# Moving 32 expert up projections ahead of the gate matrix, and all modulation chunks into the gate stage

## The chip, the cores and the metric

One core of one Trainium2 chip runs the whole program. The metric is the device time of one execution in microseconds (us).

## What is computed

Two transformer blocks run one after the other on 256 tokens of width 1024, in float32. The change touches the product-key expert layer (peer) at the end of the first block, and the modulation vectors of the second block:

```python
q = (xt @ w_q).astype(f32).reshape(T, PEER_HEADS, 2, PEER_DKEY // 2)
s1 = jnp.einsum('thd,kd->thk', q[:, :, 0], sub_k1.astype(f32))
s2 = jnp.einsum('thd,kd->thk', q[:, :, 1], sub_k2.astype(f32))
v1, i1 = lax.top_k(s1, PEER_TOPK)
v2, i2 = lax.top_k(s2, PEER_TOPK)
cand = (v1[..., :, None] + v2[..., None, :]).reshape(T, PEER_HEADS, PEER_TOPK * PEER_TOPK)
vals, ci = lax.top_k(cand, PEER_TOPK)
...
idx = jnp.take_along_axis(i1, ia, axis=-1) * PEER_NKEYS + jnp.take_along_axis(i2, ib, axis=-1)
gates = jax.nn.softmax(vals, axis=-1)
...
u = expert_u[ii]
h = jnp.einsum('tkd,td->tk', u, xx).astype(f32)
a = (jax.nn.gelu(h) * gg).astype(x.dtype)
return jnp.einsum('tk,tkd->td', a, expert_v[ii])
...
mod_x = (jax.nn.silu(c) @ w_ada[l] + b_ada[l])[:, None, :]
mod_c = (jax.nn.silu(c_ctx) @ w_ada[l] + b_ada[l])[None, None, :]
```

The kernel does not gather experts. It runs the layer densely: for each of the 128 values e of the first key, all 128 experts that share it are projected for all 256 tokens (an "up" product of 1024 by 128 experts), passed through gelu, multiplied by the gate matrix, which is zero where a token did not choose the expert, and multiplied with their value rows (a "down" product).

## The kernel before, in words

All weights come as one stream of 637 chunks of 128x1024 floats (512 KB), in a fixed order (`ORDER`). SyncE loads chunk c into slot c % 4 of the ring `RAW`; it issues a load when the chunk four places before it has been split (`lo_ready`), or, for the chunks of the modulation matrix ("ada", 72 chunks), when it has been multiplied (`chunk_done`). A chunk that is multiplied in two float32r parts is split first: ScalarE rounds it into `WH` (`split_hi`, L409), VectorE writes the rest into `WL` (`split_lo`, L786), and TensorE multiplies with three products per tile (`product`, L1316 to L1318 in a feature chunk, L1539 to L1541 in a down product). Each engine works through its own queue in program order, and semaphores join the queues. No scheduler is involved: the order is that of the code.

The stages around the change, in order of time:

- **Query stage**: 16 "wq" chunks and, between them, the key scores (L1457). VectorE does the splits of these chunks and, between them in the same loop, `top`, the top-16 searches of the first four of eight heads (`STG`, `CAND`, `IF`, `VAL` and `CIU` are its tiles). Heads 4 to 7 follow, two at a time.
- **Selection**: `EQ` compares and sums 2048 elements at a time and makes `SEL` (expert row, expert column and gate of each of 128 slots). During top-k and selection TensorE multiplies the first 40 ada chunks: two rows of conditioning vectors (`CS`) are stationary, 512 columns of weights move (L1478). ScalarE copies the sums to `MROW`, and TensorE turns them (L1486).
- **Gate stage**: `SEL` is turned and copied to `SLT`. In 32 units of 8 tokens VectorE builds one-hot matrices `OI` and `OJ` (L1061, L1064), GpSimd multiplies `OI` by the gates (L379), TensorE multiplies the two for each token (L1513), and ScalarE evicts 128x1024 to the gate matrix `G` (L580). Each unit also takes one of the last 32 ada chunks (four units to an `MROW` row).
- **Peer stage**: 128 pairs of an up chunk (24 products of 256 columns) and a down chunk (12 of 512 columns). The down sums stay in PSUM.

The four queues meet in a few lines, which the steps of the prediction name:

```python
with dve.Fori(0, 3) as it:
    step.begin(it, 11)
    for j in range(4):
        split_lo(C0["wq"] + j + 2, it, 4)
        if j:
            top(j - 1, it, 1, it * 2 + 2)
```

## Time and profile before

| | |
|---|---|
| median of 3 executions | 2290.24 us (2286.39 to 2290.87) |
| the profiled execution | 2286.94 us, its span 2285.1 us |
| mean granted TensorE clock | 0.985 of full speed |
| TensorE busy | 97% of the span |
| VectorE, ScalarE, GpSimd busy | 54%, 42%, 4% |
| chain that ended last | 88% on TensorE, 8% on VectorE |

The span runs from the first to the last instruction; the execution's own time is 1.8 us longer. Busy time of TensorE counts overlapping, pipelined products once, so a high share says that it was hardly ever without one, and not that it could not be faster. The chain is followed back from the last instruction: at each step to what released it.

### The profile page before, as it was taken

To read this page: it belongs to the slowest core of one execution; us is meant where nothing else is said; L and a number is where in the kernel's file an instruction comes from. 1 tells how busy PE (TensorE), PEld (TensorE's weight loads), DVE (VectorE), ACT (ScalarE), POOL (GpSimd) and SP (SyncE) were. 2 spreads that over 40 slices of the span, in tenths; PEclk is the share of its full clock that TensorE was granted. 3 is DMA by queue.
4 is the path that set the end of the run, shared out by engine and by line. 5 is a ranking of instruction groups with operands and counts; after the bars stand their busy time and mean duration, and the time that the engine had idled before them with its cause. 6 is when DMAs were issued, how large, how long until landed. Compare 5 with 4: busy or idle time off the path is not lost.

```text
span 2285.1 us, 37329 instructions
## 1 busy us (share of the span) xinstructions
PE 2206.0 (97%) x13410; PEld 1893.8 (83%) x13410; DVE 1242.4 (54%) x1820; ACT 956.4 (42%) x1312; POOL 92.8 (4%) x50
## 2 busy tenths in 40 slices
PE   8999898999999999999999999999899999999998
PEld 6999723559999999999998888878788889898997
DVE  4557888985555555555557433322644444255554
ACT  5644311234444444444455323212433335336653
POOL 0000002650000000000000000000000000000000
PEclk9999999999999999999999999999999999999999
DMA  6434365436555556555554322232233335254553
GB/s 215 138 131 144 113 221 194 132 129 199 187 189 184 188 188 202 187 189 184 188 189 149 111 92 92 97 100 96 70 103 100 110 111 192 91 187 146 181 188 101
DMA packets 95689, 343.14 MB, mean 150 GB/s; under 512 B 10930, under 2 KB 12594, under 8 KB 95252
## 3 DMA queue, kind: packets, MB, share of 16 engines
q1 hardware_dynamic: 94532, 337.35, 44.4%
q0 software_dynamic: 1104, 5.05, 0.7%
q8 instruction: 38, 0.62, 0.1%
q14 instruction: 15, 0.12, 0.0%
HBM read 341.31 MB, written 1.05 MB: 150 GB/s over the span
## 4 chain that ended last, share of the span: by engine, by line
PE 88%; DVE 8%; issue 2%; ACT 1%; DMA 0%; DVEq 0%; POOL 0%; ACTq 0%; POOLq 0%
PE ps L1316 19%; PE ps L1317 19%; PE ps L1318 19%; PE ps L1539 5%; PE ps L1540 5%; PE ps L1541 5%; PE ps L1513 3%; PE ps L1478 3%; PE ps L1347 2%; PE ps L1348 2%; PE ps L1349 2%; PE ps L1671 1%; PE ps L1356 1%; DVE WL L786 1%; PE ps L1720 1%
## 5 line engine op out<-in xcount | busy, mean ns | idle before, releaser
L786 DVE TENSOR_TENSOR WL<-RAW,WH 128x1024 fp32r<-128x1024 f32 x565 | 683.2, 1224 | 665.1 <-ACT WH L409 661.0
L1316 PE MATMUL ps<-XH,WH 128*128 128x256 f32 (+1 forms) x2648 | 803.2, 303 | 29.7 <-DVE WL L786 16.2
L409 ACT ACTIVATE WH<-RAW 128x1024 fp32r<-128x1024 f32 x565 | 586.4, 1055 | 538.2 <-PE ps L1318 342.1
L1317 PE MATMUL ps<-XL,WH 128*128 128x256 f32 (+1 forms) x2648 | 794.5, 300 | 0.0
L1318 PE MATMUL ps<-XH,WL 128*128 128x256 f32 (+1 forms) x2648 | 794.2, 300 | 0.0
L1316 PEld LDWEIGHTS ps<-XH,WH 128*128 128x128 f32 x2648 | 511.8, 193 | 58.0 <-issue 20.5
L1317 PEld LDWEIGHTS ps<-XL,WH 128*128 128x128 f32 x2648 | 512.8, 194 | 20.3 <-issue 1.2
L1318 PEld LDWEIGHTS ps<-XH,WL 128*128 128x128 f32 x2648 | 512.5, 194 | 14.5
L1539 PE MATMUL ps<-WH,AH 128*128 128x512 f32 x512 | 200.8, 392 | 0.0
L1540 PE MATMUL ps<-WH,AL 128*128 128x512 f32 x512 | 200.7, 392 | 0.0
L1541 PE MATMUL ps<-WL,AH 128*128 128x512 f32 x512 | 199.2, 389 | 0.0
L1478 PE MATMUL ps<-RAW,CS 128*2 128x512 f32 x288 | 131.6, 601 | 4.6 <-ACTq L556 3.8
L1316 PE MATMUL ps<-HIDH,WH 128*128 (+2 forms) x352 | 119.3, 339 | 4.3 <-DVE HIDL L1158 4.3
L1318 PE MATMUL ps<-HIDH,WL 128*128 (+2 forms) x352 | 118.8, 337 | 0.0
L1317 PE MATMUL ps<-HIDL,WH 128*128 (+2 forms) x352 | 118.8, 337 | 0.0
L1541 PEld LDWEIGHTS ps<-WL,AH 128*128 128x128 f32 x512 | 96.2, 188 | 21.0
L1539 PEld LDWEIGHTS ps<-WH,AH 128*128 128x128 f32 x512 | 96.6, 189 | 16.7
L1540 PEld LDWEIGHTS ps<-WH,AL 128*128 128x128 f32 x512 | 96.7, 189 | 15.3
L1154 DVE TENSOR_TENSOR HT<-TA,ps 128x512 f32<-128x512 f32 (+1 forms) x44 | 24.4, 555 | 141.7 <-PE ps L1318 138.6
L1478 PEld LDWEIGHTS ps<-RAW,CS 128*2 128x2 f32 x288 | 21.6, 84 | 87.9 <-issue 68.2
L379 POOL TENSOR_TENSOR OI<-OI,SLT 128x1024 f32<-128x1024 f32 x32 | 86.5, 2702 | 124.9 <-DVE OI L1061 124.9
L1513 PEld LDWEIGHTS ps<-OI,OJ 128*128 128x128 f32 x512 | 61.1, 196 | 36.7 <-issue 36.7
(255 smaller groups left out, 2257.4 us busy)
## 6 DMA issues: line engine op xcount, KB each, us to landing
RAW<-in_wstream SPq DMA_DIRECT2D x637, 512.0 KB, 3.8
H<-in_xT SPq DMA_DIRECT2D x1, 1024.0 KB, 4.8
CTX<-in_ctxT POOLq DMA_DIRECT2D x1, 1024.0 KB, 7.6
HX<-in_ctxT POOLq DMA_DIRECT2D x1, 1024.0 KB, 5.9
DIST<-in_dist POOLq DMA_DIRECT2D x1, 1024.0 KB, 5.2
out<-HX SPq DMA_DIRECT2D x2, 512.0 KB, 3.3
MASK<-in_mask POOLq DMA_DIRECT2D x1, 512.0 KB, 3.9
DFTL<-in_dftl POOLq DMA_DIRECT2D x1, 512.0 KB, 3.7
```

Source lines behind the costliest of these rows:

```text
L379: pool.tensor_tensor(OI[:, q, :, :], OI[:, q, :, :], SLT[:, 2, bass.ds(it * 16 + 8 * q, 8)].unsqueeze(2).to_broadcast([P, 8, P]), ALU.mult ...
L409: act.activation(WH[:, slot, :], RAW[:, slot, :], ACT.Copy).then_inc(hi_ready, 1)
L786: dve.tensor_tensor(WL[:, slot, :], RAW[:, slot, :], WH[:, slot, :].bitcast(F32), ALU.subtract).then_inc(lo_ready, 1)
L1316: pe.matmul(dst, wh, xh, start=start, stop=False, skip_group_check=not check)
L1317: pe.matmul(dst, wh, xl, start=False, stop=False, skip_group_check=not check)
L1318: return pe.matmul(dst, wl, xh, start=False, stop=stop, skip_group_check=not check)
L1347: pe.matmul(dst, xh[:, k, t], WH[:, slot, w], start=(k == 0), stop=False)
L1478: ins = pe.matmul(ps[0:2, bank, :], CS[:, k, :], RAW[:, c % 4, kk * 512:kk * 512 + 512], start=(k == 0), stop=(k == KB - 1))
L1513: ins = pe.matmul(ps[:, 2 * q + t // 4, (t % 4) * P:(t % 4) * P + P], OJ[:, q, t, :], OI[:, q, t, :], start=True, stop=True)
L1539: pe.matmul(dst, AH[:, e % 2, t], WH[:, c % 4, d], start=first, stop=False)
L1540: pe.matmul(dst, AL[:, e % 2, t], WH[:, c % 4, d], start=False, stop=False)
L1541: ins = pe.matmul(dst, AH[:, e % 2, t], WL[:, c % 4, d], start=False, stop=last)
```

## The change

The stream gets a new part, "pre", between "wq" and "ada": the up chunks of rows 96 to 127. TensorE multiplies them during top-k and selection (`pre_up`), and ScalarE puts the gelu of each straight into its row of `G`. In the gate stage ScalarE evicts only rows 0 to 95, and VectorE multiplies the evicted sums of rows 96 to 127 into what `G` holds there (`gated_rows`). In the peer stage 32 down chunks come first, without ups, and then 96 pairs.

The splits of 14 wq chunks and 32 pre chunks leave VectorE for GpSimd. The multiplication of `OI` by the gates leaves GpSimd: VectorE builds `OI` in eight instructions per unit that compare and multiply in one.

All 72 ada chunks stand in the first 30 of the 32 gate units. The conditioning vectors are padded to 32 columns, and the eight products of a row go in turn to four groups of 32 PSUM partitions (each group holds two of the eight). After every fourth chunk the 128x512 sums are copied, turned by four full transposes (`turn_row`) and the four groups are added (`row_sum`).

```diff
-ADA1 = 10
-ADA2 = MODB // 4 - ADA1
-ADA_EXP = 6
-UNITS = T // 8 // ADA2
+PRE = 32
+PRE_ROW = NKEYS - PRE
+NE = NKEYS - PRE
+UNITS = T // 8
+ADA_UNITS = UNITS - 2
...
     ("wq", 16),
+    ("pre", PRE),
     ("ada", MODB),
-    ("peer", 256),
+    ("peer", 256 - PRE),
...
+def ada_through(n):
+    return min(MODB, (n + 1) * MODB // ADA_UNITS)
+def turn_after(done):
+    return done // 4 - 1 if done >= 6 and done % 4 == 2 else None
...
-            with pool.Fori(0, T // 16) as it:
-                for q in range(2):
-                    pool.wait_ge(s["oi_ready"], at(q + 1, 2, it))
-                    pool.tensor_tensor(OI[:, q, :, :], OI[:, q, :, :],
-                                       SLT[:, 2, bass.ds(it * 16 + 8 * q, 8)].unsqueeze(2).to_broadcast([P, 8, P]),
-                                       ALU.mult).then_inc(s["gi_ready"], 1)
-            pool.wait_ge(chunk_done, C0["peer"] + 3 + 2 * 63 + 1)
+            pool.wait_ge(s["pool_consts"], 4)
+            pool.memset(CS[:, :, :], 0.0).then_inc(s["cs_zeroed"], 1)
+            pool.wait_ge(lo_ready, C0["wq"] + 2)
+            for c in range(C0["wq"] + 2, ADA):
+                pool.wait_ge(hi_ready, c + 1)
+                pool.tensor_tensor(WL[:, c % 4, :], RAW[:, c % 4, :], WH[:, c % 4, :].bitcast(F32),
+                                   ALU.subtract).then_inc(lo_ready, 1)
...
+            for i in range(PRE):
+                c = C0["pre"] + i
+                if i and c + 2 < ADA:
+                    split_hi(c + 2)
+                act.wait_ge(chunk_done, c + 1)
+                act.activation(G[:, PRE_ROW + i, :], ps[:, (U_PRE + i) % 4, 0:T],
+                               ACT.Gelu_apprx_tanh).then_inc(ring_evac, 1)
+                if i == 20:
+                    act.wait_ge(s["vals_ready"], 1)
+                    act.activation(VAL[:, :, :, :], VAL[:, :, :, :], ACT.Exp).then_inc(s["val_exp"], 1)
+                if i == PRE - 5:
+                    act.wait_ge(s["slots_turned"], 1)
+                    act.activation(SLT[:, 0:2, :], ps[:, 4, :].rearrange("p (a t) -> p a t", t=T), ACT.Copy)
+                    act.activation(SLT[:, 2, :], ps[:, 5, 0:T], ACT.Copy).then_inc(s["slots_ready"], 1)
...
+            for n in range(UNITS):
+                act.wait_ge(s["onehot_used"], n + 3)
+                act.activation(G[:, 0:PRE_ROW, 8 * n:8 * n + 8],
+                               ps[:, 2 * (n % 2):2 * (n % 2) + 2, :].rearrange("p b (t i) -> p i (b t)", t=4)[:, 0:PRE_ROW, :],
+                               ACT.Copy).then_inc(s["g_ready"], 1)
+                while done < MODB // 4 and ada_through(n) >= 4 * done + 4:
+                    act.wait_ge(chunk_done, ADA + 4 * done + 4)
+                    if done >= 2:
+                        act.wait_ge(s["row_turned"], done - 1)
+                    act.activation(MROW[:, done % 2, :], ps[:, 6 + done % 2, :], ACT.Copy).then_inc(s["mrow_ready"], 1)
+                    done += 1
...
             with dve.Fori(0, 3) as it:
                 step.begin(it, 11)
-                for j in range(4):
-                    split_lo(C0["wq"] + j + 2, it, 4)
-                    if j:
-                        top(j - 1, it, 1, it * 2 + 2)
+                for part in range(3):
+                    top(part, it, 1, it * 2 + 2)
                 step.end(3)
-            split_lo(ADA - 2)
-            split_lo(ADA - 1)
...
+            def onehots(n):
+                q, tok = n % 2, slice(8 * n, 8 * n + 8)
+                if n < 2:
+                    dve.wait_ge(chunk_done, ADA - 1 + n)
+                else:
+                    dve.wait_ge(s["onehot_used"], n + 1)
+                dve.tensor_tensor(OJ[q][:, :, :], IOTA[:, :].unsqueeze(1).to_broadcast(wide),
+                                  SLT[:, 1, tok].unsqueeze(2).to_broadcast(wide), ALU.is_equal)
+                for t in range(8):
+                    own = slice(8 * n + t, 8 * n + t + 1)
+                    ins = dve.tensor_scalar(OI[q][:, t, :], IOTA[:, :], SLT[:, 0, own], SLT[:, 2, own],
+                                            ALU.is_equal, ALU.mult)
+                ins.then_inc(s["onehot_ready"], 1)
+            def gated_rows(n):
+                dve.wait_ge(s["g_ready"], n + 3)
+                g = G[:, PRE_ROW:NKEYS, 8 * n:8 * n + 8]
+                rows = ps[:, 2 * (n % 2):2 * (n % 2) + 2, :].rearrange("p b (t i) -> p i (b t)", t=4)
+                dve.tensor_tensor(g, rows[:, PRE_ROW:NKEYS, :], g, ALU.mult).then_inc(s["gm_ready"], 1)
+            def row_sum(g):
+                dve.wait_ge(s["row_turned"], g + 1)
+                turned = ps[:, 5, :].rearrange("p (i r c) -> p i r c", i=4, r=4)
+                dve.tensor_reduce(MOD[:, 4 * g:4 * g + 4, :], turned[:, :, :, 0:2].rearrange("p i r c -> p i c r"),
+                                  AXX, ALU.add).then_inc(s["row_summed"], 1)
+            dve.sem_inc(s["gm_ready"], 2)
+            onehots(0)
+            dve.wait_ge(ring_evac, U_GATES)
+            for n in range(UNITS):
+                if n + 1 < UNITS:
+                    onehots(n + 1)
+                gated_rows(n)
+                if n >= 1:
+                    for done in range(ada_through(n - 2) + 1 if n >= 2 else 1, ada_through(n - 1) + 1):
+                        if turn_after(done) is not None:
+                            row_sum(turn_after(done))
...
+            def pre_up(i, it=None):
+                bank_free(U_PRE + i, it)
+                feature_chunk(C0["pre"] + i, ps[:, (U_PRE + i) % 4, 0:T], XH, XL, it, 4)
+            with pe.Fori(0, PRE // 4 - 1) as it:
+                for i in range(4):
+                    pre_up(i, it)
             pe.wait_ge(s["sc_ready"], 16 + 4)
-            def mod_chunk(c, j, bank, it=None, n=0):
-                pe.wait_ge(landed[c % 4], at(16 * (c // 4 + 1), 4 * n, it))
-                for kk in range(2):
-                    k = 2 * j + kk
-                    ins = pe.matmul(ps[0:2, bank, :], CS[:, k, :], RAW[:, c % 4, kk * 512:kk * 512 + 512],
-                                    start=(k == 0), stop=(k == KB - 1))
-                ins.then_inc(chunk_done, 1)
-            def turn_rows(rows, m0, count):
-                for i in range(count):
-                    m = m0 + i
-                    ins = pe.transpose(ps[:, 7, 2 * m:2 * m + 2], rows[0:2, i * P:i * P + P], ID2[:, :])
-                return ins
-            with pe.Fori(0, ADA1 // 2) as it:
-                for q in range(2):
-                    pe.wait_ge(s["mrow_ready"], at(q + 1, 2, it))
-                    for j in range(4):
-                        mod_chunk(ADA + 4 * q + j, j, 6 + q, it, 8)
-            pe.wait_ge(s["id2_ready"], 1)
-            pe.wait_ge(s["mrow_ready"], ADA1 + 2)
-            turn_rows(MROW, 0, 4 * ADA1)
             pe.wait_ge(s["sel_ready"], 1)
             for n in range(3):
                 for tt in range(TT):
                     ins = pe.transpose(ps[:, 4 + n // 2, (n % 2) * T + tt * P:(n % 2) * T + tt * P + P],
-                                       SEL[:, n, tt, :, :].rearrange("p h k -> p (h k)"), IDENT[:, :])
+                                       SEL[:, n, tt, :, :].rearrange("p h k -> p (h k)"), IDP[:, :])
             ins.then_inc(s["slots_turned"], 1)
+            for i in range(PRE - 4, PRE):
+                pre_up(i)
+            def mod_chunk(i):
+                c, bank = ADA + i, 6 + (i // 4) % 2
+                pe.wait_ge(landed[c % 4], 16 * (c // 4 + 1))
+                for kk in range(2):
+                    k = 2 * (i % 4) + kk
+                    rows = slice(32 * (k % 4), 32 * (k % 4) + 32)
+                    ins = pe.matmul(ps[rows, bank, :], CS[:, k, :], RAW[:, c % 4, kk * 512:kk * 512 + 512],
+                                    start=(k < 4), stop=(k >= 4))
+                ins.then_inc(chunk_done, 1)
+            def turn_row(g):
+                pe.wait_ge(s["mrow_ready"], g + 1)
+                if g:
+                    pe.wait_ge(s["row_summed"], g)
+                for i in range(4):
+                    ins = pe.transpose(ps[:, 5, i * P:i * P + P], MROW[:, g % 2, i * P:i * P + P], IDP[:, :])
+                ins.then_inc(s["row_turned"], 1)
+            pe.wait_ge(s["cs_ready"], 1)
+            pe.wait_ge(s["const_landed"], 16 * 11)
+            pe.wait_ge(ring_evac, U_GATES)
             pe.sem_inc(s["onehot_used"], 2)
-            with pe.Fori(0, ADA2) as it:
-                for u in range(UNITS):
-                    q = u % 2
-                    pe.wait_ge(s["oj_ready"], at(u + 1, UNITS, it))
-                    pe.wait_ge(s["gi_ready"], at(u + 1, UNITS, it))
-                    pe.wait_ge(s["g_ready"], at(u + 1, UNITS, it))
-                    for t in range(8):
-                        ins = pe.matmul(ps[:, 2 * q + t // 4, (t % 4) * P:(t % 4) * P + P], OJ[:, q, t, :],
-                                        OI[:, q, t, :], start=True, stop=True)
-                    ins.then_inc(s["onehot_used"], 1)
-                    if u == 0:
-                        pe.wait_ge(s["mrow_ready"], at(ADA1 + 2, 1, it))
-                    if u % (UNITS // 4) == 0:
-                        j = u // (UNITS // 4)
-                        mod_chunk(ADA + 4 * ADA1 + j, j, 6, it, 4)
-            pe.wait_ge(s["mrow_ready"], MODB // 4 + 2)
-            turn_rows(MROW2, 4 * ADA1, 4 * ADA2).then_inc(s["mod_turned"], 1)
+            done = 0
+            for n in range(UNITS):
+                q = n % 2
+                pe.wait_ge(s["onehot_ready"], n + 1)
+                pe.wait_ge(s["g_ready"], n + 1)
+                pe.wait_ge(s["gm_ready"], n + 1)
+                for t in range(8):
+                    ins = pe.matmul(ps[:, 2 * q + t // 4, (t % 4) * P:(t % 4) * P + P], OJ[q][:, t, :], OI[q][:, t, :],
+                                    start=True, stop=True)
+                ins.then_inc(s["onehot_used"], 1)
+                while done < ada_through(n):
+                    if done >= 8 and done % 4 == 0:
+                        pe.wait_ge(s["mrow_ready"], done // 4 - 1)
+                    mod_chunk(done)
+                    done += 1
+                    if turn_after(done) is not None:
+                        turn_row(turn_after(done))
+            turn_row(MODB // 4 - 1)
...
             pe.wait_ge(s["mod_ready"], 1)
+            down(0, 0, PC + 2, first=True)
+            with pe.Fori(0, PRE // 4 - 1) as it:
+                for i in range(1, 5):
+                    down(i, i, PC + 2 + i, it, 4)
+            for i in range(PRE - 3, PRE):
+                down(i, i, PC + 2 + i)
             def pair(e, it=None):
                 if e >= 2:
                     pe.wait_ge(s["gated_ready"], at(e - 1, 4, it))
-                up(e + 2, PC + 2 + 2 * e, it)
-                down(e, PC + 3 + 2 * e, it, first=it is None and e == 0)
+                up(e + 2, PQ + 2 + 2 * e, it)
...
+    parts += [up[PRE_ROW:NKEYS]]
+    parts += [tokens(x["w_ada_2"][0][:, n:n + 512]) for n in range(0, N_MOD * D, 512)]
+    order = [up[0:1], up[1:2], down[PRE_ROW:NKEYS]]
+    for e in range(NE):
+        if e + 2 < NE:
```

**VectorE, the loop over the first heads.** Before, in the loop body (L786 is a split, L962 to L993 are steps of `top`):

```order
148 L785 REGISTER_ALU
149 L786 TENSOR_TENSOR WL<-RAW,WH 128x1024
150 L962 MAX V_102<-STG_101 128x8 x4
151 L105 REGISTER_ALU
152 L966 MAX_INDEX I_103<-V_102,STG_101 128x8 x4
153 L969 TENSOR_TENSOR CAND<-V_102 128x256 x2
```

Now:

```order
144 L996 MAX V_101<-STG_100 128x8 x4
145 L117 REGISTER_ALU
146 L1000 MAX_INDEX I_102<-V_101,STG_100 128x8 x4
147 L1003 TENSOR_TENSOR CAND<-V_101 128x256 x2
148 L117 REGISTER_ALU
149 L1008 ISA
150 L1008 COPY IF<-I_102 128x4x16
```

The split that stood ahead of the second search is gone from this queue, and so are the other three of each round. They stand on GpSimd, where before there was the product of `OI`:

```order
13 L384 MEMSET CS 128x256 [waits pool_consts]
14 L390 TENSOR_TENSOR WL<-RAW,WH 128x1024 [waits hi_ready,lo_ready]
15 L390 TENSOR_TENSOR WL<-RAW,WH 128x1024 [waits hi_ready] x45
16 L394 DMA CTX<-in_ctxT 128x2048 [waits chunk_done]
```

GpSimd now has 46 splits in a row, one behind the other, with nothing between them but the wait for ScalarE's half.

**TensorE, the gate stage.** Before, one turn of the loop, four units (L1513 one-hots, L1478 an ada chunk):

```order
1299 L1513 MATMUL ps<-OI,OJ 128x128 x8
1300 L1518 REGISTER_ALU
1301 L1475 ISA
1302 L1478 MATMUL ps<-RAW,CS 2x512 x2
1303 L1509 REGISTER_ALU
1304 L1513 MATMUL ps<-OI,OJ 128x128 x8
1305 L1478 MATMUL ps<-RAW,CS 2x512 x2
```

Now, units 2 to 4 (L1602 one-hots, L1578 ada chunks, two products each, L1588 the transposes of a row of sums):

```order
1493 L1602 MATMUL ps<-OI_118,OJ_116 128x128 x8
1494 L1578 MATMUL ps<-RAW,CS 32x512 x4
1495 L1588 MATMUL ps<-IDP,MROW 128x128 x4
1496 L1578 MATMUL ps<-RAW,CS 32x512 x2
1497 L1602 MATMUL ps<-OI_119,OJ_117 128x128 x8
1498 L1578 MATMUL ps<-RAW,CS 32x512 x4
1499 L1602 MATMUL ps<-OI_118,OJ_116 128x128 x8
```

Each unit has two or three chunks in place of one, and on average 0.6 groups of four transposes.

## Rows read from the trace of the kernel before

**Rows 1.** The page, busy time of the engines.

```profile
PE 2206.0 (97%) x13410; PEld 1893.8 (83%) x13410; DVE 1242.4 (54%) x1820; ACT 956.4 (42%) x1312; POOL 92.8 (4%) x50
```

**Rows 2.** Windows by stage: PE, PEld, DVE, ACT, POOL busy (count), PE clock, DMA share, GB/s.

```profile
219.70:296.20 76.50, 62.45 (x448) 59.99 (x448) 63.37 (x241) 31.61 (x59) 0.24 (x1) 0.90 0.29 96
296.20:343.60 47.40, 46.62 (x103) 8.81 (x104) 42.63 (x225) 6.63 (x10) 0.00 (x0) 0.95 0.76 257
343.60:372.80 29.20, 27.48 (x98) 7.16 (x96) 28.68 (x18) 2.34 (x4) 0.00 (x0) 1.00 0.86 301
372.80:379.80 7.00, 1.54 (x6) 1.14 (x6) 4.24 (x4) 0.87 (x2) 2.68 (x1) 0.50 0.00 0
379.80:507.50 127.70, 123.77 (x640) 69.25 (x640) 112.56 (x62) 37.46 (x41) 83.78 (x31) 0.99 0.38 127
```

**Rows 3.** Chain of waits, first copy of the two double rounds.

```profile
297.21 0.43 DVE STG L948
...
320.15 0.43 DVE STG L948
```

**Rows 4.** Groups by line and form, VectorE from 216 to 375 us.

```profile
L786 DVE TENSOR_TENSOR WL<-RAW,WH 128x1024 fp32r<-128x1024 f32 x14 | 16.9, 1224 | 3.2 <-ACT WH L409 1.4 <-DVE CIU L998 1.0
L1037 DVE TENSOR_TENSOR EQ<-IAF,IOTA 128x2048 f32<-128x2048 f32 x4 | 9.2, 2292 | 0.1
...
L969 DVE TENSOR_TENSOR CAND<-V 128x256 f32<-128x256 f32 x16 | 5.8, 413 | 0.0
...
L948 DVE COPY STG<-SC 128x512 f32 x7 | 2.8, 423 | 5.9 <-ACT SC L526 4.8 <-DVE CIU L998 1.1
```

**Rows 5.** Timeline, start of one head's round and of the next, VectorE.

```profile
250.24 0.42 DVE L948 COPY STG<-SC 128x512 f32 x1
...
267.30 0.42 DVE L948 COPY STG<-SC 128x512 f32 x1
```

**Rows 6.** Timeline, the key scores behind two wq chunks, TensorE.

```profile
228.56 0.61 PE L1457 MATMUL ps<-K12T,QT 128*128 128x128 f32 x4
231.88 0.61 PE L1457 MATMUL ps<-K12T,QT 128*128 128x128 f32 x4
```

**Rows 7.** Timeline of the gate stage's start, VectorE and GpSimd.

```profile
375.62 1.23 DVE L1061 TENSOR_TENSOR OI<-IOTA,SLT 128x1024 f32<-128x1024 f32 x1 [2.76 <-ACT SLT L574]
376.77 1.22 DVE L1064 TENSOR_TENSOR OJ<-IOTA,SLT 128x1024 f32<-128x1024 f32 x1
377.06 2.68 POOL L379 TENSOR_TENSOR OI<-OI,SLT 128x1024 f32<-128x1024 f32 x1 [85.58 <-DVE OI L1061]
377.90 2.92 DVE L1061 TENSOR_TENSOR OI<-IOTA,SLT 128x1024 f32<-128x1024 f32 x1
```

**Rows 8.** Timeline of two gate units, TensorE.

```profile
383.31 1.88 PE L1478 MATMUL ps<-RAW,CS 128*2 128x512 f32 x4
385.12 2.05 PE L1513 MATMUL ps<-OI,OJ 128*128 128x128 f32 x16
387.10 1.45 PE L1478 MATMUL ps<-RAW,CS 128*2 128x512 f32 x3
```

**Rows 9.** Timeline, products of 64 rows in two halves of the array.

```profile
100.17 2.82 PE L1397 MATMUL ps<-VT,KT 64*128 64x128 f32 x32
```

**Rows 10.** Timeline, from the last gate unit to the first up product.

```profile
505.08 1.02 ACT L580 ACTIVATE G<-ps 128x1024 f32 x1 [2.95 <-PE ps L1513]
...
507.39 3.99 ACT L409 ACTIVATE WH<-RAW 128x1024 fp32r<-128x1024 f32 x4
...
512.26 0.55 PE L1316 MATMUL ps<-XH,WH 128*128 128x256 f32 x1 [2.41 <-DVE WL L786]
```

**Rows 11.** Timeline, one pair of the peer stage: up, down, next up.

```profile
806.41 0.28 PE L1316 MATMUL ps<-XH,WH 128*128 128x256 f32 x1
...
809.28 0.40 PE L1539 MATMUL ps<-WH,AH 128*128 128x512 f32 x1
...
812.03 0.28 PE L1316 MATMUL ps<-XH,WH 128*128 128x256 f32 x1
```

More of the change, by code:

```diff
@@ L567, in _ @@
-            act.wait_ge(s["vals_ready"], 1)
-            act.activation(VAL[:, :, :, :], VAL[:, :, :, :], ACT.Exp).then_inc(s["val_exp"], 1)
-            for g in range(ADA_EXP, ADA1):
-                mod_rows(g)
-            act.wait_ge(s["slots_turned"], 1)
-            act.activation(SLT[:, 0:2, :], ps[:, 4, :].rearrange("p (a t) -> p a t", t=T), ACT.Copy)
-            act.activation(SLT[:, 2, :], ps[:, 5, 0:T], ACT.Copy).then_inc(s["slots_ready"], 1)
-            act.sem_inc(s["g_ready"], 2)
@@ L620, in _ @@
             tmp_c, xh_c = TMP16[:, :, C_], XH2_16[:, :, C_]
-            for e in range(CTX_E, 126):
+            for e in range(CTX_E, NE - 2):
                 pair(e)
@@ L1115, in _ @@
             tmp_c = TMP16[:, :, C_]
-            for e in range(CTX_E, 126):
+            for e in range(CTX_E, NE - 2):
                 pair(e)
@@ L1530, in up, with down @@
                 feature_chunk(c, ps[:, e % 4, 0:T], XH, XL, it, 8)
-            def down(e, c, it=None, first=False, last=False):
-                split_ready(c, it, 8)
-                pe.wait_ge(s["a_lo"], at(e + 1, 4, it))
+            def down(e, p, c, it=None, n=8, first=False, last=False):
+                split_ready(c, it, n)
+                pe.wait_ge(s["a_lo"], at(p + 1, 4, it))
                 for tt in range(TT):
@@ L1561, in _ @@
                     pair(e, it)
-            for e in range(CTX_E, 126):
+            for e in range(CTX_E, NE - 2):
                 if e == CTX_E + 3:
@@ L1567, in _ @@
                     norm_sum(N_CTX1, TMP16[:, :, C_])
-            down(126, PC + 254)
-            down(127, PC + 255, last=True)
+            down(NE - 2, NKEYS - 2, C0["up1"] - 2)
+            down(NE - 1, NKEYS - 1, C0["up1"] - 1, last=True)
             def context_up(j):
```

212 lines of the change are left out of this document (109 added, 103 removed).

## The prediction

> **What bounds the kernel now.** The page first [rows 1]: TensorE is busy for 97% of the span, so only what shortens its work, or a stretch in which it follows another engine, can pay. The windows by stage show such a stretch [rows 2]. From 219.7 to 296.2 us the 16 wq chunks run, and TensorE is busy for 62.5 of 76.5 us although a chunk with its scores needs 3.32 us where nothing holds it [rows 6]: 16 of them would take 53. VectorE is busy for 63.4 us there. One round of its loop, one head's search and four splits, takes 17.06 us [rows 5], of which the splits are 4 x 1.22 [rows 4]. From 296.2 to 372.8 us VectorE is busy for 71 of 76.6 us with top-k and selection; TensorE fills the time with 40 ada chunks and would be through earlier. So up to 372.8 us, when `SEL` is there, the end is set by VectorE. In the gate stage (379.8 to 507.5 us) TensorE sets the pace: 3.79 us from one unit's ada products to the next one's [rows 8], of which GpSimd and VectorE need less. Then it is TensorE without a gap in the peer stage, 677 us: 2.87 us for an up, 2.75 us for a down [rows 11].
>
> **What the change takes away.** 32 up chunks leave the peer stage: 32 x 2.87 = 91.8 us, all of it on the path [rows 11]. The 32 downs that remain alone need 2.75 us each on TensorE; behind each stand one split (1.0 us on ScalarE [rows 10], 1.22 us on VectorE [rows 4]) and two short operations of 0.4 us, and a load at 0.5 MB per 2.75 us, 191 GB/s, where 301 were reached [rows 2]. So they stay covered, with about 1 us to spare on VectorE, the first to show if that cover were gone.
>
> **Until `SEL`, without a new wait.** VectorE starts its first round at 250.24 - 17.06 = 233.2 us. Without splits a round is 17.06 - 4.88 = 12.2 us, a double round 22.9 us [rows 3], and from the end of top-k (320.15 + 22.9 = 343.1) to 372.8 there are 29.7 us. 233.2 + 48.8 + 45.9 + 29.7 = 357.6 us. TensorE is as far: second wq chunk at 228.9, 14 x 3.32 to 275.4, 28 pre chunks of 2.87 to 355.8 us. Behind `SEL` it now has six transposes (1.54 us), then the last four pre chunks (11.5 us, some 1.5 more because its clock was low, as the 0.50 before 379.8 us shows), and VectorE's first one-hots wait for the third of them. The gate stage starts 14.5 us after `SEL`, where it was 7.0: at 372.1 us, 7.7 before today's 379.8.
>
> **The new wait: GpSimd and VectorE get in each other's way.** GpSimd's product starts at 377.06 and ends at 379.74 us [rows 7]. VectorE's compare, issued at 377.90, takes 2.92 us in place of 1.23: it ends 1.08 us after GpSimd does, so it stood still for GpSimd's whole operation. The Trainium skill, "SBUF — State Buffer", section "Who interferes with whom", says the same of any VectorE instruction with two SBUF inputs, adds copies and casts in a two-port mode, and has the one that comes second block for the whole instruction. Now GpSimd runs 46 such operations in a row while VectorE searches. Three things must be chosen.
>
> How long one split holds VectorE: the rows bound it [rows 7]. At most 2.70 us; at least 377.99 to 379.74 = 1.75 us, if GpSimd itself first stood behind VectorE's `OJ`. I take 2.3, between them and nearer to the row as it stands. (The skill's "GPSIMD Engine Reference", section "Performance versus the Vector engine", has 4497 ns for 2048 elements; half is 2.25, an estimate by that page.)
>
> Which operations wait: two-input ones surely. The copy of 512 elements takes 423 ns and the addition of 256 takes 413 [rows 4]; a copy goes two elements at a time, so I count copies and casts as well. That makes six per round (`STG`, two `CAND`, `IF`, `VAL`, `CIU`) and twelve per double round; the searches have one input and do not wait.
>
> How long they wait, at 2.70: to 275.4 us GpSimd is busy 2.70 of each 3.32 us. A lone operation finds it so 81% of the time and waits half of 2.70, so 1.1 us; a round is 12.2 + 6.6 = 18.8 us, 2.24 rounds are done. Then splits come without a gap. Three operations per round stand right behind another and let a split in between, a full 2.70; three wait 1.3. A round is 24.2 us, the last 1.76 end at 318.0. A double round would be 51.1 us. But ScalarE, after chunk 20 of pre, waits for the end of top-k (`vals_ready`), and behind that wait are its splits from chunk 23 on. GpSimd, from about 225 us on, ends chunk 22, its 37th, after 37 x 3.05 us (0.35 for the VectorE operation that stands ahead of it), at 338. By then 9.0 us of the double rounds' 45.9 are done; the rest ends at 374.9. In selection each group of three big operations (2.3 us each) takes 3.1 us more, the second compare a whole split, the next first one the rest of another; seven splits for 3.5 groups, 11 us. `SEL` is there at 374.9 + 29.7 + 11 = 415.6, the gate stage starts at 430.1: 50 us late. The same steps at 1.75 (15.0 to 15.7 us a round, 29.9 a double round, GpSimd at TensorE's pace through with chunk 22 at 335, 6 us in selection) give `SEL` at 385.3 and 20 us late. At 2.3 it is **+37 us**.
>
> **The gate stage.** One-hots with the change to and from ada products take 3.79 - 4 x 0.43 = 2.07 us per unit (0.43: the first three of four passes in 1.88 - 0.59 [rows 8]). 32 units: 66.2. The transposes of 18 rows, four passes of 0.11 and 0.2 for the change, 11.5. From the last one-hots to the first up, ScalarE evicts (0.8 for three quarters of 1.02 [rows 10]), splits (1.0) and VectorE splits (1.22): 3.3. The ada products are 72 x 2 x 2 passes. One behind the other they are 288 x 0.43 = 123.8 us. Neighbouring products now go to different groups of 32 columns, and no row of before shows such groups. Nearest is a product on 64 rows whose halves change after every fourth product: 32 passes in 2.82 us, 0.09 each [rows 9], against (2.05 - 0.27)/16 = 0.11 on the full array [rows 8]. Halves overlap where they change, so I let the second pass of a product run beside the first of the next: a product costs 0.43 and each of 30 bursts one more, 174 x 0.43 = 74.8. Sum 155.8 us; before, 379.8 [rows 2] to 512.26 [rows 10] is 132.4: **+23 us**. Without overlap 204.8, +72.
>
> The Trainium skill, "TensorE: Matmul & The Clock Gate", section "Part 3: Packing small matmuls — row/col tiling", reports 2.38 times the speed for three column tiles. No row here shows that; an estimate by that page is 123.8 / 2.38 = 52 us for the ada products.
>
> VectorE needs per unit 1.22 for `OJ`, eight compares of 128 elements at some 0.2, 0.4 for the rows of G, 0.2 for a sum: 3.4 of 4.8 us. The DMA delivered 40 chunks in 72.3 us, 1.81 each; here one comes every 2.1 us. Neither bounds.
>
> **Sum.** +37 + 23 - 92 = -32 us. Against the profiled execution (span 2285.1, its own time 2286.9) that is 2255; the median of the runs lies 3.3 above it, so I say 2256.
>
> **Rivals.**
> - *The column groups do not run beside each other.* The gate stage is then 205 us: 37 + 72 - 92 = +17, 2304 us, slower. For it: the moving data of one product already comes at 0.43 us per 512 columns, and each group needs its own; rows 9 show rows, not columns. Against: rows 9 show overlap at all. It decides if less than about a third of the 49 us comes back. 20%; with the lightest port waits it would be no change.
> - *The port costs little*, because short VectorE operations slip between two splits or copies are free: between no wait, -8, and two-input operations alone at 2.70, +26 (same steps: `SEL` at 391.5). With -8: 2286.9 - 8 + 23 - 92 = 2210. For it: operations of 0.2 us; against: rows 7. 13%.
> - *The waits in the gate stage chain up.* `turn_row` waits for the sum of the row before, which VectorE does behind the eviction of the next unit. If each of 18 costs 1 us, +18: 2274. 8%.
>
> - *All four groups run together.* The ada products then fit between the loads, and the DMA sets the stage: 72 x 1.81 + 3.3 = 134 us, +1. 37 + 1 - 92 = -54, 2233 us. For it: the groups share no output rows; against: the passes of one product go to one group, one behind the other. 10%.
>
> My forecast, with its waits between +20 and +50, has 49% and its own range 2238 to 2272.
>
> **How the numbers follow.** A difference of up to 0.2% (4.6 us) could not be told from none. The range reaches to the rival without waits at the bottom and to the serial groups at the top: 2210 to 2304. Faster: the forecast, the last three rivals, and the serial groups where the port is cheap, 79%; same 5%; slower, serial groups at the forecast's waits or worse, 16%.
>
> **What will show it.** `STG` and `CAND` with means well above 0.42 and 0.41 us, `SEL` at 385 to 416; ScalarE waiting for `vals_ready` and GpSimd idle from about 336 until then. In the gate stage starts of ada passes a few ns apart and a period of 4.8 us; 6.4 would mean serial groups. A peer stage of 586 us. I am wrong if `SEL` comes before 372.8, or if the gate stage follows another engine than TensorE.

## The result: 2222.3 us, 2.9% faster, twice the gain that was forecast

| | before | changed |
|---|---|---|
| median of 4 executions | 2288.57 us (2286.39 to 2290.87) | 2222.28 us (2220.16 to 2226.48) |
| the profiled execution, its span | 2286.94, 2285.1 us | 2223.94, 2222.2 us |
| mean granted TensorE clock | 0.985 | 0.985 |

The ratio is 0.9712, 95% interval 0.9693 to 0.9732. Forecast were 2256 us and a sum of -32 us against the profiled execution; measured are -63.0. The sign is right and 2222 lies inside 2210 to 2304, but not inside the forecast's own range, 2238 to 2272. The case that came true is the last rival, "all four groups run together", to which I had given 10%; its 2233 us are 9 too high against the profiled execution.

| stage | before | forecast | changed |
|---|---|---|---|
| one-hots of the gate stage start at | 379.8 | 416.8 (+37) | 408.7 (+28.8) |
| from there to the first up product | 132.4 | 155.8 (+23) | 134.05 (+1.6) |
| from there to the end of the span | 1772.9 | -91.8 | 1679.4 (-93.5) |

28.8 + 1.6 - 93.5 = -63.1 us; the spans differ by 62.9. A third of the 31 us that the forecast missed lies ahead of the gate stage and in the peer stage (8 and 2), two thirds in the gate stage.

### The profile page after: what moved, and what is told of

The parts are those of the page before. It is cut to its first block, busy times and chain, and to the rows that moved or that the text cites. A ratio compares the mean times of both kernels' runs of the same rounds, so it can differ in the third digit from the quotient of the medians.

```text
span 2222.2 us, 37167 instructions
## 1 busy us (share of the span) xinstructions
PE 2130.7 (96%) x13410; PEld 1880.4 (85%) x13410; DVE 1212.6 (55%) x2016; ACT 951.1 (43%) x1312; POOL 126.1 (6%) x65
## 3 DMA queue, kind: packets, MB, share of 16 engines
HBM read 341.24 MB, written 1.05 MB: 154 GB/s over the span
## 4 chain that ended last, share of the span: by engine, by line
PE 85%; DVE 10%; issue 2%; ACT 2%; DMA 2%; DVEq 0%; ACTq 0%; SPq 0%
PE ps L1398 18%; PE ps L1399 18%; PE ps L1400 18%; PE ps L1629 5%; PE ps L1630 5%; PE ps L1631 5%; PE ps L1429 2%; PE ps L1431 2%; PE ps L1430 2%; PE ps L1602 2%; PE ps L1578 2%; DMA RAW<-in_wstream 1%; PE ps L1769 1%; DVE EQ L1069 1%; PE ps L1438 1%
## 5 line engine op out<-in xcount | busy, mean ns | idle before, releaser
L820 DVE TENSOR_TENSOR WL<-RAW,WH 128x1024 fp32r<-128x1024 f32 x519 | 627.2, 1224 | 601.3 <-ACT WH L419 597.7
L1400 PEld LDWEIGHTS ps<-XH,WL 128*128 128x128 f32 x2648 | 511.7, 193 | 14.5
L390 POOL TENSOR_TENSOR WL<-RAW,WH 128x1024 fp32r<-128x1024 f32 x46 | 119.5, 2608 | 91.7 <-ACT WH L419 91.6
L697 ACT ACTIVATE HIDH<-HT 128x256 f32 (+2 forms) x44 | 23.1, 525 | 158.4 <-DVE HT L1236 158.4
L1429 PE MATMUL ps<-WH,XH 128*128 128x512 f32 x208 | 82.3, 396 | 3.7 <-DVE WL L820 3.7
L1430 PE MATMUL ps<-WH,XL 128*128 128x512 f32 x208 | 82.0, 394 | 0.0
```

Of the source, the lines that this page charges most:

```text
L390: pool.tensor_tensor(WL[:, c % 4, :], RAW[:, c % 4, :], WH[:, c % 4, :].bitcast(F32), ALU.subtract).then_inc(lo_ready, 1)
L820: dve.tensor_tensor(WL[:, slot, :], RAW[:, slot, :], WH[:, slot, :].bitcast(F32), ALU.subtract).then_inc(lo_ready, 1)
L1400: return pe.matmul(dst, wl, xh, start=False, stop=stop, skip_group_check=not check)
L1429: pe.matmul(dst, xh[:, k, t], WH[:, slot, w], start=(k == 0), stop=False)
L1430: pe.matmul(dst, xl[:, k, t], WH[:, slot, w], start=False, stop=False)
```

## The profile after

The windows by stage (PE, PEld, DVE, ACT, POOL busy with counts, PE clock, DMA share, GB/s), which answer to [rows 2]:

```profile
220.60:278.50 57.90, 57.23 (x448) 55.38 (x448) 44.42 (x175) 30.03 (x54) 38.27 (x16) 0.97 0.41 136
278.50:360.00 81.50, 68.73 (x563) 68.31 (x563) 75.71 (x280) 40.26 (x59) 56.29 (x23) 0.94 0.43 144
360.00:393.00 33.00, 14.71 (x113) 13.90 (x112) 32.55 (x16) 5.72 (x9) 20.23 (x6) 0.81 0.31 105
393.00:408.70 15.70, 14.80 (x103) 14.65 (x103) 3.70 (x11) 4.30 (x8) 4.76 (x2) 0.83 0.20 68
408.70:542.70 134.00, 126.19 (x872) 75.38 (x873) 114.10 (x331) 39.12 (x53) 0.00 (x0) 1.00 0.83 283
```

TensorE now works through the wq chunks almost without a gap (57.2 of 57.9 us). They end at 278.5 us, 3.1 later than the prediction's 3.32 us a chunk had it. Then TensorE is idle for 13 us of the next 81.5, and again for 18 us of the 33 before `SEL` (392.9). In the gate stage the DMA moves 283 GB/s, where it moved 127 in [rows 2]. That column was the one to look at: the stage has gone from one chunk every 3.8 us to 72 chunks in 134 us, one every 1.86.

VectorE by line and form from 216 to 375 us, against [rows 4], and behind it the same kernel's selection (353.4 to 393.2 us):

```profile
L1003 DVE TENSOR_TENSOR CAND<-V 128x256 f32<-128x256 f32 x16 | 13.7, 907 | 0.0
L1008 DVE CAST IF<-I 128x64 uint32 x7 | 7.1, 1040 | 0.7 <-DVE CAND L1003 0.2
L982 DVE COPY STG<-SC 128x512 f32 x7 | 6.1, 900 | 10.1 <-ACT SC L536 8.0 <-DVE CIU L1032 2.2
L1031 DVE COPY VAL<-CV 128x32 f32 x7 | 4.5, 639 | 0.6
...
L1069 DVE TENSOR_TENSOR EQ<-EQ,IF 128x2048 f32<-128x2048 f32 x4 | 15.3, 3822 | 0.1
L1067 DVE TENSOR_TENSOR EQ<-IAF,IOTA 128x2048 f32<-128x2048 f32 x4 | 13.4, 3340 | 0.1
L1071 DVE TENSOR_REDUCE SEL<-EQ 128x128 f32<-128x2048 f32 x4 | 9.1, 2286 | 0.1
```

These are means. The two-input `CAND` needed 413 ns and now takes 907; the copy `STG` went from 423 to 900 and the cast `IF`, 64 elements wide, to 1040. So copies and casts wait too. The reduction, with one input, still takes 2286 ns while GpSimd works beside it: it does not wait for GpSimd. Now one split of GpSimd in the middle of the pre chunks, with VectorE's rows after it, and the end of GpSimd's pause, with ScalarE's exponential and the first of the big compares:

```profile
305.55 2.40 POOL L390 TENSOR_TENSOR WL<-RAW,WH 128x1024 fp32r<-128x1024 f32 x1 [0.48 <-ACT WH L419]
307.33 4.12 DVE L1003 TENSOR_TENSOR CAND<-V 128x256 f32<-128x256 f32 x4
311.60 2.17 DVE L1008 CAST IF<-I 128x64 uint32 x1
...
352.62 0.42 ACT L576 ACTIVATE VAL<-VAL 128x256 f32<-128x256 f32 x1 [9.36 <-DVE VAL L1056]
...
353.49 2.29 DVE L1067 TENSOR_TENSOR EQ<-IAF,IOTA 128x2048 f32<-128x2048 f32 x1
354.06 15.09 POOL L390 TENSOR_TENSOR WL<-RAW,WH 128x1024 fp32r<-128x1024 f32 x4 [11.54 <-ACT WH L419]
355.81 4.33 DVE L1069 TENSOR_TENSOR EQ<-EQ,IF 128x2048 f32<-128x2048 f32 x1
```

A split takes 2.40 us, and ahead of each GpSimd pauses for 0.48 us, until ScalarE has the half for it; the period is 2.88 us, that of TensorE's ups. A VectorE operation that comes during a split waits for its end, and one that comes in the pause does not wait. The four `CAND` in 4.12 us took 0.90, 0.41, 2.62 and 0.41: the first ended 0.28 us after the split of 305.55, the second passed through the pause, the third began 0.07 us after the next split (308.43) and stood behind all of it. Of the 48 `STG`, `CAND`, `IF`, `VAL` and `CIU` operations of top-k 17 waited, 23.9 us together, and the other 31 took their old time. The pause from 342.5 to 354.1 is the one that the prediction placed at 336, behind `vals_ready`. In the selection four splits take 15.09 us, 3.8 each, and five of the eight compares and products 4.3 to 4.4 in place of 2.29: each engine stands behind the other in turn.

TensorE at the start of the gate stage and some units later, to be held against [rows 8]:

```profile
408.66 2.02 PE L1602 MATMUL ps<-OI,OJ 128*128 128x128 f32 x16 [0.82 <-DVE OI L1099]
410.61 1.06 PE L1578 MATMUL ps<-RAW,CS 128*32 128x512 f32 x8
411.62 2.05 PE L1602 MATMUL ps<-OI,OJ 128*128 128x128 f32 x16
...
425.57 1.05 PE L1578 MATMUL ps<-RAW,CS 128*32 128x512 f32 x4
426.56 0.66 PE L1588 MATMUL ps<-IDP,MROW 128*128 128x128 f32 x4
427.14 2.25 PE L1578 MATMUL ps<-RAW,CS 128*32 128x512 f32 x8
```

Eight passes, two whole chunks, take 1.06 us; before, four passes took 1.88. Four passes take 1.05 too: a chunk alone costs as much as two that come together. The eight passes at 427.14 took 2.25 us, because the second of the two chunks had not landed (its weight load waited 1.05 us for the DMA).

## Experiments: what do the column groups do, and what sets the gate stage?

Theory A: products of four different groups run together, and the loads set the stage. Rivals: loads alone matter, whatever the groups; only neighbouring products overlap (rival C, the prediction's model); VectorE sets the pace. "Stage" is the time from the first one-hots to the first up product of the peer stage.

**e1, one group.** The row sums take this group alone.

```diff
-                    rows = slice(32 * (k % 4), 32 * (k % 4) + 32)
+                    rows = slice(0, 32)
...
-                                    start=(k < 4), stop=(k >= 4))
+                                    start=(k == 0), stop=(k == 7))
```

> All 144 modulation products go to the same 32 output partitions (the row sums then take that one group); nothing else changes. Theory A, in the changed kernel products of four different column groups run together: without that each of the 288 passes costs 0.43 us again, the gate stage is 66 + 124 + 12 + 3 = 205 us in place of 134, the time 2224 + 71 = 2295 us. Rival B, the loads set the gate stage and the passes lie beside them: 134 us and 2224 us whatever the groups.

Measured 2295.2 us (ratio 1.0024, 1.0014 to 1.0034), gate stage 204.05 us: theory A, to 1 us. TensorE (the same kinds of rows as above):

```profile
413.53 3.62 PE L1578 MATMUL ps<-RAW,CS 128*32 128x512 f32 x8
417.08 2.05 PE L1602 MATMUL ps<-OI,OJ 128*128 128x128 f32 x16
```

Without groups the whole change would be worth nothing. The serial sum of the prediction, 204.8 us for this stage, is thereby tested too: one-hots, row transposes, tail and 0.43 us a pass were right as a sum.

**e2, two groups.** `rows` from `k % 2`, the flags and the row sums to suit.

> The products alternate between two groups of 32 columns in place of four, so each product still goes to another group than its neighbours. Theory A, as many products run together as there are different groups: two chunks take some 4 x 0.43 = 1.8 us in place of 1.06, 36 times 0.75 is 27 us on TensorE, gate stage 161 us if TensorE sets it, less if loads or VectorE leave room, time 2240 to 2251 us. Rival C, the model of the prediction, in which only neighbouring products overlap: two groups are worth as much as four, gate stage 134 us, time 2224 us.

Measured 2232.75 us (0.975, 0.9734 to 0.9767), stage 142.5 us.

```profile
421.51 1.91 PE L1578 MATMUL ps<-RAW,CS 128*32 128x512 f32 x8
423.35 2.05 PE L1602 MATMUL ps<-OI,OJ 128*128 128x128 f32 x16
425.33 1.05 PE L1578 MATMUL ps<-RAW,CS 128*32 128x512 f32 x4
```

Eight passes in 1.91 us, against 3.62 with one group and 1.06 with four: as many products run together as there are groups. The single passes show it: with four groups (the burst at 410.61) the four first passes start within 21 ns and the four second ones 0.45 us later; with two, passes start in pairs at 421.51, 421.96, 422.39 and 422.82; with one, singly every 0.43 us. Rival C is refuted. The time is 7 us under theory A's lowest figure: TensorE had 25 us more of ada passes (69.9 for the 44.6 of e8, below), but the stage grew by 8.5 only, since part of it filled what TensorE had waited for loads.

**e3, half loads.** Each of these loads brings the first 512 of 1024 columns, so the output is computed from old data in part.

```diff
-                    load((ADA + 4 + j) % 4, it * 4 + (ADA + 4 + j))
+                    sp.dma_start(RAW[:, (ADA + 4 + j) % 4, 0:512],
+                                 a["wstream"][it * 4 + (ADA + 4 + j)][:, 0:512]).then_inc(landed[(ADA + 4 + j) % 4], 16)
```

> Of each modulation chunk (and of the first peer chunks behind them) only the first half of the columns is loaded, the products read all the same; a load moves 256 KB. Theory D, the DMA sets the gate stage: it falls from 134 us to what TensorE's own work needs, 32 x 2.05 + 36 x 1.1 + 18 x 0.66 = 117 plus changes, so about 122 us and 2212 us. Rival P, TensorE and the one-hots set it and the loads are only just hidden: it falls by no more than the 12 us that TensorE waited for landings, in all likelihood by under 4: 2220 us or more.

**e4, half the scaled one-hots.** `for t in range(8)` becomes `range(0, 8, 1 if n < 2 else 2)`; four of eight tokens of a unit keep old one-hots, from the third unit on.

> From the third unit on VectorE makes only four of the eight scaled one-hots of a unit (the other four keep their old values), so its work per unit falls from about 3.6 to 2.3 us. Theory V, VectorE sets the pace of the gate stage: 134 us falls to the bound of the loads (72 x 1.75 = 126) or of TensorE, 6 to 10 us, time 2214 to 2218 us. Rival D or P, loads or TensorE set it: under 3 us, time above 2220 us.

**e8, both together**, with the parts left out as in e3 and e4.

> Half loads and half the scaled one-hots together: neither the DMA nor VectorE can set the gate stage, what is left is TensorE's own work and its changes between kinds. Theory A: half loads alone gave 123.1 us with 18 us of short waits for one-hots, so the stage falls to 117 to 120 us, time 2206 to 2209 us. Rival B, something else holds it (the evictions of ScalarE, the turns of the rows): 122 to 123 us, 2212 us.

Measured: e3 2211.97 us (0.9661, 0.9645 to 0.9677), stage 123.05, as theory D had it; e4 2221.89 (0.9701, 0.9685 to 0.9717), stage 133.0, against theory V; e8 2211.31 (0.9659, 0.9644 to 0.9674), stage 120.2. The stage of e8 is as theory A had it, its time is not, because its gate stage started 3.7 us later than that of e3. TensorE's ada products in the changed kernel and in e8, whole stage:

```profile
L1578 PE MATMUL ps<-RAW,CS 128*32 128x512 f32 x288 | 56.0, 604 | 2.9 <-DMA RAW<-in_wstream 2.7
```

```profile
L1578 PE MATMUL ps<-RAW,CS 128*32 128x512 f32 x288 | 44.6, 605 | 0.0
```

So the loads hold the stage for 11 us (134.05 to 123.05), and most of that does not show as idle time but as bursts that got longer (56.0 for 44.6). VectorE, though 85% busy, was not seen to hold it with full loads: the 133.0 of e4 lies within the 131.8 to 134.05 of the kernels whose gate stage is the changed one's (the changed kernel, e5, e6, e7). Once the loads are out of the way VectorE is worth 2.9 us, little more than that scatter. What is left in e8 is 120.2 us, and TensorE waits for hardly anything there; less 66.2, 11.5 and 3.3 of the prediction's sum that leaves 39.2 us for the ada products, for which the prediction had 74.8.

Half loads do not tell the DMA's speed from the depth of the ring. In the changed kernel's stage SyncE waited 87.3 us, in 51 waits, for a chunk to be multiplied before it could issue a load, and the DMA engines were busy for 83%. So whether the DMA's speed or the four slots of the ring set the 1.75 us a chunk (the 72 of them start between 410.6 and 534.6 us) stays open; no run had more slots.

## Experiments: the port

**e5, no splits on GpSimd.** `pool.tensor_tensor(WL...)` becomes `pool.sem_inc(lo_ready, 1)`; the low halves of 46 chunks are old ones.

> GpSimd's 46 splits of the wq and pre chunks are left out (TensorE multiplies old low halves; GpSimd only counts). Theory A, those splits hold VectorE up through the shared port: without them SEL comes at about 357.6 us, the prediction's own sum without waits, in place of 392.9, and the gate stage starts near 372 in place of 408.7: 2186 us. The copies STG and the additions CAND are back at 0.42 and 0.41 us from 0.90 and 0.91. Rival B, VectorE's rounds are longer for another reason (it waits for scores, or for its own results): SEL stays within 5 us of 392.9, 2218 us or more.

Measured 2186.5 us (0.955, 0.9536 to 0.9565); `SEL` at 358.5, gate stage at 371.98 us, against 357.6 and 372.1 in the prediction. VectorE, as above:

```profile
L1002 DVE TENSOR_TENSOR CAND<-V 128x256 f32<-128x256 f32 x16 | 5.8, 414 | 0.0
L981 DVE COPY STG<-SC 128x512 f32 x7 | 2.8, 425 | 10.7 <-ACT SC L535 8.6 <-DVE CIU L1031 2.2
L1007 DVE CAST IF<-I 128x64 uint32 x7 | 1.2, 195 | 0.7 <-DVE CAND L1002 0.2
```

GpSimd's splits hold VectorE up, by 34.4 us at `SEL`; its waits for scores stay as they were (8.6 us for 8.0), and what is left is the sum without waits to 1 us. The selection starts at 353.5 instead of 329.3 us, 24.2 us for 39 splits, 0.62 each, which are the 23.9 us of the 17 operations that waited. It takes 39.4 instead of 29.2, 10.2 us for seven splits, 1.5 each. Over all 46 that is 0.75 us a split, less than the 1.22 that VectorE needs to do one itself; in the selection it is more.

**e6, ScalarE waits for top-k later** (`if i == 20:` becomes `if i == PRE - 6:`).

> ScalarE waits for the end of top-k behind pre chunk 26 in place of chunk 20, so that six of the seven splits that fell into the selection are done during top-k. Theory A, a split costs VectorE more in the selection (seven cost 10 us there) than in top-k (39 splits made top-k some 25 us longer than the sum without waits, 0.6 each): SEL comes 10 x 6/7 - 6 x 0.6 = 5 us earlier, 2217 us. Rival B, a split holds VectorE for the same time wherever it falls: 2222 us within 1.5.

Measured 2220.53 us (0.9705, 0.9692 to 0.9718), not to be told from the changed kernel (0.9712). It misses A's 2217 us and lies within B's 1.5 us. In the profile two splits fall into the selection in place of seven, and it is 6.2 us shorter. Top-k ends 4.2 us later, and `SEL` comes 2.0 us earlier (390.9). These two show nothing: in the changed kernel, e1 to e4 and e8, whose code ahead of `SEL` is the same, the selection took 39.4 to 39.5 us every time, but it started anywhere from 351.4 to 355.9, and `SEL` came from 390.9 to 395.3. That a split costs more in the selection rests on e5, not on e6. The same 4 us of scatter lie in every start of a gate stage in this document.

## Experiments: can the idle time before SEL be used?

**e7, 40 ups before the gate stage** (`PRE = 40`, and e6's line).

> 40 up projections are made during top-k in place of 32, and ScalarE waits for top-k behind chunk 34 of them. TensorE stood still for 31 us before SEL in the changed kernel. Theory A: 8 x 2.87 = 23 us leave the peer stage and fill that time; eight more splits hold VectorE for 0.6 to 1.4 each, less what the later wait gives: 2222 - 23 + 3 = 2202 us, SEL at 393 to 398. Rival B, TensorE becomes the bound before SEL: 36 ups of 2.88 from 278.5 end at 382, before SEL, so that this costs nothing unless SEL comes before 382. Rival C, the splits near SEL hold the selection up as they did (1.4 us each, and the last four ups wait for them): 2222 - 23 + 12 = 2211 us.

Measured 2207.54 us (0.9645, 0.963 to 0.9659). Behind the first up of the peer stage 23.5 us are gone (1655.9 for 1679.4), as all had it. The gate stage starts 8.4 us later (417.1). The selection, which in e7 takes 45.7 us:

```profile
L1067 DVE TENSOR_TENSOR EQ<-IAF,IOTA 128x2048 f32<-128x2048 f32 x4 | 17.6, 4388 | 0.1
L1069 DVE TENSOR_TENSOR EQ<-EQ,IF 128x2048 f32<-128x2048 f32 x4 | 17.4, 4355 | 0.1
```

All eight big operations wait for a split. That is rival C in kind, with 8 us of a price where C had 12 and A 3; the time lies between A's 2202 and C's 2211.

**e9, ada chunks ahead of SEL.** They need no split. All 32 ups stand before `SEL`; twelve ada chunks fill TensorE's wait, four follow the transposes, 56 stay in the gate stage at two a unit.

```diff
-            with pe.Fori(0, PRE // 4 - 1) as it:
+            with pe.Fori(0, PRE // 4) as it:
                 for i in range(4):
                     pre_up(i, it)
...
+            for i in range(12):
+                mod_chunk(i)
             pe.wait_ge(s["sel_ready"], 1)
...
-            for i in range(PRE - 4, PRE):
-                pre_up(i)
+            for i in range(12, 16):
+                mod_chunk(i)
```

ScalarE copies the first two rows of sums ahead of the slots, `turn_row` comes every 1.67 units from the first one on, and e6's line is in it.

> All 32 up projections are made before SEL; twelve modulation chunks follow them while TensorE waits for SEL, four more come behind the transposes, and the gate stage spreads the other 56; ScalarE waits for top-k behind pre chunk 26. Theory A: the gate stage starts 7 to 8 us behind SEL, as in the kernel before, in place of 15.6 (8 us less); with 56 chunks its loads need 56 x 1.75 = 98 us and no longer bind, so it takes what the run with half loads and half one-hots shows, 120.2, less 16 x 0.53 = 112, or VectorE's 32 x 3.55 = 114; SEL at 391. 2220.5 - 8 - 19 = 2193 us. Rival B, short waits between VectorE's one-hots, ScalarE's evictions and TensorE keep the stage at the 123 us of the run with half loads: 2202 us.

Measured **2199.05 us** (0.9603, 0.959 to 0.9617), the lowest median of the kernels that leave nothing out: 4.0% under the kernel before, 1.0% under the changed one. The gate stage starts 5.5 us behind `SEL` (398.95) and takes 117.45 us. TensorE's waits for VectorE's one-hots, 395 to 525 us, and the stage in one row:

```profile
PEld ps L1627 <- DVE OI L1122: 20.3, 25, 1.4
...
PE ps L1627 <- DVE OI L1122: 5.1, 10, 1.1
```

```profile
398.90:516.40 117.50, 104.80 (x810) 71.89 (x809) 113.10 (x331) 37.83 (x51) 0.00 (x0) 1.00 0.75 265
```

VectorE is busy for 113.1 of 117.5 us and TensorE waits for its one-hots: with 16 of the 72 loads gone it looks like the next bound, between A's 114 and B's 123. This is read from the waits; no run made VectorE's work shorter here. Another 3 us over the forecast lie at the end of the program, where the granted clock was 0.98 in place of 0.99 over 280 us.

**e10, 36 ups, eight and eight ada chunks**; **e11, 40 ups, four and four**; **e12, 36 ups, four and four.** Only these numbers differ from e9.

> The same with 36 up projections, eight modulation chunks ahead of SEL and eight behind the transposes. Theory A: 4 x 2.87 = 11.5 us less in the peer stage; each further split that falls into the selection holds VectorE (forty made SEL 8.7 us later than 32, so four 4.3 us); 2 to 3 us later at the gate stage, since four of the eight chunks behind the transposes wait for their loads. 2193 - 11.5 + 4.3 + 2.5 = 2188 us. Rival B, TensorE, through with 36 ups at 382 and with eight chunks at 392, is late for SEL: 2193 us or more.

> The same with 40 up projections, four modulation chunks ahead of SEL and four behind it, 64 in the gate stage. Theory A: 40 ups end at 278.5 + 40 x 2.88 = 394, with waits for splits in the selection near 402, when SEL comes; the gate stage starts 8 to 10 us behind SEL and takes 64 x 1.75 = 112 to 118 us. Against the run with 40 ups (2207.5: stage 133.3, start 15.5 behind SEL) 6 and 15 us less: 2187 us. Rival B, the last splits end after SEL and hold the end of the ups: 2195 us.

> 36 up projections, four modulation chunks ahead of SEL and four behind it, 64 in the gate stage. Theory A: what held the run with 36 ups and sixteen early chunks is the loads behind the ups (its transposes came 5 us after SEL and the first one-hots 18.5 after it); with eight early chunks the transposes follow SEL (397.4) at once and the gate stage starts 7 to 8 us behind it, at 405; it takes 120 to 126 us (the loads of 64 chunks, 118.7 with 56 and 126.1 with 64), and the rest 1666.6 us: 2193 to 2199 us. Rival B, the loads of the four chunks behind SEL and of those in the first units hold it the same way: 2202 us or more.

Measured: e10 2203.73 us (0.9626, 0.9613 to 0.9639), e11 2200.1 (0.9613, 0.9599 to 0.9626), e12 2201.12 (0.961, 0.9597 to 0.9624). None beats e9 (e11 and e12 cannot be told from it), and all miss theory A; e10 and e11 lie in the open ranges of their rivals B, e12 between its two. e10 starts its gate stage 18.5 us behind `SEL`, because TensorE was still at its loads:

```profile
396.76 4.54 PE L1592 MATMUL ps<-RAW,CS 128*32 128x512 f32 x12 [2.62 <-DMA RAW<-in_wstream]
401.54 1.05 PE L1592 MATMUL ps<-RAW,CS 128*32 128x512 f32 x4 [0.23 <-DMA RAW<-in_wstream]
402.52 0.87 PE L1604 MATMUL ps<-IDP,SEL 128*128 128x128 f32 x6
```

The transposes, queued behind them, come 5 us after `SEL` (397.4). In e11 they come 5.2 us after `SEL` (403.4), because the ups, which had waited 9.2 us for splits, ended at 406.8; its stage, with 64 chunks, took 126.1 us. e12 takes that away (start at 403.7, 6.1 behind `SEL`), but its stage, with 64 chunks, took 127.6 us, with TensorE waiting for loads again. Every up put ahead of `SEL` gives 2.9 us and costs about 1 in splits; every ada chunk left in the gate stage costs up to 1.75. The two compete for the same idle 31 us, and the four kernels end within 5 us of each other.

## Why the prediction was half wrong

**The step that failed** is the one on overlap in the gate stage: "I let the second pass of a product run beside the first of the next: a product costs 0.43 and each of 30 bursts one more, 174 x 0.43 = 74.8", against the rival for reason of "the passes of one product go to one group, one behind the other". In fact the first passes of four products of different groups start within 21 ns, and their second passes 0.45 us later (e1 and e2 show the same with one and two groups). A burst of up to four products costs two steps of 0.43, not five. 39.2 us in place of 74.8 took TensorE below the loads, and then "here one comes every 2.1 us. Neither bounds" failed as well: the DMA's 72 x 1.81 + 3.3 = 134 us, the figure of the last rival, was the length of the stage (134.05; e3 shows that it is the loads for 11 us of it). That the two agree to 0.1 us is luck. The 1.81 was read where TensorE itself needed 4 x 0.43 = 1.72 us a chunk, so it was no measure of the loads; in e10, where TensorE had nothing but loads to wait for, twelve chunks from 396.76 us on came 1.65 us apart. And the 134.05 are 2.0 us ahead of the first chunk, 124.0 from the first chunk to the last (1.75 each) and 8.1 behind the last one's start. The Trainium skill, "TensorE: Matmul & The Clock Gate", "Part 3: Packing small matmuls — row/col tiling", has 2.38 times for three column tiles, from which came the prediction's estimate of 52 us. It was nearer than the 74.8, and this trace agrees with it in kind: here two groups give 1.88 times (131.5 to 69.9 us) and four 2.95 (to 44.6, in bursts that are one or two chunks long).

**The port: mechanism right, price 10 us too high.** The sum without waits is confirmed to 1 us (e5), and copies and casts do wait, down to 32 elements. A split took 2.40 us, near the 2.3 that I chose for the hold. But "then splits come without a gap" was wrong, and with it that all six operations of a round wait: GpSimd paused 0.48 us in every 2.88, and 31 of the 48 passed. A waiting operation ends with its split, so the one or two behind it run in the pause. That is what the second rival had for it, short operations that slip between two splits; its other reason, that copies are free, is out. The splits cost 34.4 us at `SEL` in place of 45 (416.8 - 372.1); `SEL` without waits came 1 us later than worked out, and from there to the one-hots it was another 1 us (15.7, forecast 14.5). The selection's stall, 11 us at 2.70 and 6 at 1.75, was 10.2. A slip that changed little: the double round's 51.1 us at 2.70 do not follow from the rule given, which makes 46.9 and moves the end of top-k by under 1 us. `SEL` at 392.9 was in the bounds, 385 to 416.

**The peer stage: right.** -93.5 for -91.8. The downs alone stayed covered. Its length was misread, though: from the first up to the last down it is 725 us before and 630 after, not 677 and 586 (its own 2.87 + 2.75 us make 719 for 128 pairs); no term of the sum rested on that.

**"I am wrong if the gate stage follows another engine than TensorE"**: it followed the loads.

**The rivals.** Serial groups are out (e1). The cheap port, between -8 and +26 us, missed the measured +28.8 by less than the scatter of `SEL`. The turns of rows did not chain: 1.5 us of waits for `MOD` in the whole stage. The forecast itself, 2256, has a slip of 2 us: its 2255 plus the 3.3 that it names would be 2258.

## What to carry to other kernels

When a change may make an engine two or three times faster in a stage, work out at once the floors of all others there (loads above all) and give the case in which they bind its full chance; the rows before showed 301 GB/s at a DMA share of 0.86, and 72 chunks in the stage's old 132.4 us ask for 285. Small products of different column groups want to be issued next to each other, with all their data landed. And moving work to GpSimd beside a busy VectorE is not free: here it cost 0.6 us per split beside many short operations and 1.5 beside long two-input ones, where VectorE needs 1.22 for a split.

## What the runs showed of the hardware

- With 32-column outputs, 128x512 f32: 8 passes take 3.62 us in one group, 1.91 in two, 1.06 in four; 4 passes in two groups take 1.05.
- GpSimd's 128x1024 subtraction takes 2.40 us beside VectorE's short operations and about 3.8 next to its 2048-element ones, which take 4.3 to 4.4 in place of 2.29 where they wait; a reduction of 2048 elements is untouched.
- A VectorE operation that waited for GpSimd's split took up to 2.6 us in place of 0.41 (`CAND`), and ended 0.04 to 0.28 us after the split; a cast of 64 elements took 1040 ns on average in place of 195.
- VectorE's 128x128 compare-and-multiply with two per-partition scalars takes 0.34 us, and the next one starts 0.26 us after it, not the "some 0.2" of the prediction.
